# Eight of the 24 modulation slabs move from the first block's attention to the second block's projection

## What is computed

```python
for i in range(DEPTH):                       # DEPTH = 2, dm = 1024
    mod = jax.nn.silu(c) @ mod_w[i] + mod_b[i]          # 1024 x 6144 weights
    modc = jax.nn.silu(c_ctx) @ mod_w[i] + mod_b[i]
    sh1, sc1, g1, sh2, sc2, g2 = jnp.split(mod[:, None, :], 6, axis=-1)
...
    hx = _modulate(_rmsnorm(x, ln1_g[i]), sh1, sc1)
    hc = _modulate(_rmsnorm(ctx, ln1_g[i]), sh1c, sc1c)
    yx, yc = _mixer_ab(...) if i % 2 == 0 else _mixer_cd(...)
    x = x + g1 * yx
    hx = _modulate(_rmsnorm(x, ln2_g[i]), sh2, sc2)
    x = x + g2 * _moe(hx, ...)
```

## Time and profile before

| | |
|---|---|
| median of three runs | 2252.05 us (2248.34 to 2257.75) |
| profiled execution, its own time | 2249.79 us |
| its span | 2248.1 us |
| PE busy | 2137.4 us, 95% |
| DVE busy | 1087.9 us, 48% |
| ACT busy | 613.4 us, 27% |
| DMA | 629.97 MB, mean 280 GB/s |
| first block's attention | about 124 to 223 us |
| second block's projection | about 851 to 905 us |
| second block's attention | about 908 to 946 us |

### The profile page before, as it was taken

How to read it: one execution, slowest core, us unless ns; L and a number is a source line. 1 busy time by engine, 2 the same in 40 slices (tenths; PEclk the granted TensorE clock), 3 DMA queues, 4 the chain that set the end, 5 groups by cost and what they waited for, 6 DMA issues and landing times.

```text
span 2248.1 us, 32119 instructions
## 1 busy us (share of the span) xinstructions
PE 2137.4 (95%) x12440; PEld 1388.0 (62%) x12440; DVE 1087.9 (48%) x1969; ACT 613.4 (27%) x1214; POOL 12.7 (1%) x20
## 2 busy tenths in 40 slices
PE   7999999999999889889999999999999999999998
PEld 4744644444343347564444444478989989898997
DVE  5677541111111136642222222167888777787876
ACT  4446532112121114431111111133451012434001
POOL 0000000000000010000000000000000000000000
PEclk9999999999999999999999999999999999999999
DMA  8189169998999994229999999952345546235452
GB/s 349 76 360 427 75 253 378 386 383 352 429 392 429 428 386 184 113 91 384 427 429 429 428 429 428 427 243 104 140 170 187 187 153 255 110 114 206 181 190 98
DMA packets 50146, 629.97 MB, mean 280 GB/s; under 512 B 5888, under 2 KB 6912, under 8 KB 11904
## 3 DMA queue, kind: packets, MB, share of 16 engines
q1 hardware_dynamic: 45008, 611.30, 66.7%
q10 hardware_dynamic: 2880, 9.44, 1.0%
q0 software_dynamic: 2160, 7.87, 0.9%
HBM read 614.42 MB, written 14.16 MB: 280 GB/s over the span
## 4 chain that ended last, share of the span: by engine, by line
PE 71%; DMA 15%; DVE 10%; ACT 2%; issue 2%; SPq 1%; DVEq 0%; ACTq 0%
PE ps L1908 10%; DMA ring<-in_ex_gate 7%; PE ps L1847 7%; DMA ring<-in_ex_up 6%; PE ps L1376 6%; PE ps L1378 6%; PE ps L1377 6%; PE ps L1987 4%; PE ps L1989 4%; PE ps L1988 4%; PE ps L1924 3%; PE ps L1803 3%; PE ps L1881 2%; PE ps L1723 1%; PE ps L1399 1%
## 5 line engine op out<-in xcount | busy, mean ns | idle before, releaser
L1908 PE MATMUL ps<-ring,E 128*64 128x512 f32 x1152 | 260.1, 609 | 16.7 <-DMA ring<-in_ex_up 14.4
L1378 PE MATMUL ps<-hn_hi,w_lo 128*128 128x256 f32 x928 | 262.4, 283 | 0.0
L1847 PE MATMUL ps<-ring,E 128*64 128x512 f32 x992 | 221.1, 598 | 10.5 <-DMA ring<-in_ex_gate 7.5
L1908 PEld LDWEIGHTS ps<-ring,E 128*64 128x64 f32 x1152 | 87.9, 140 | 185.6 <-issue 185.6
L2736 DVE TENSOR_TENSOR E<-E,ps 128x512 f32<-128x512 f32 x18 | 12.4, 688 | 354.3 <-PE ps L1908 354.3
L1378 PEld LDWEIGHTS ps<-hn_hi,w_lo 128*128 128x128 f32 x928 | 177.8, 192 | 0.0
L1847 PEld LDWEIGHTS ps<-ring,E 128*64 128x64 f32 x992 | 73.8, 138 | 142.3 <-issue 142.1
L1102 ACT ACTIVATE hT<-ps 128x512 f32<-128x512 f32 x70 | 41.9, 599 | 370.1 <-PE ps L1803 370.1
L1376 PE MATMUL ps<-hn_hi,w_lo 128*128 128x256 f32 x480 | 138.3, 288 | 1.7 <-DVE w_lo L2838 1.7
L1377 PE MATMUL ps<-hn_lo,w_lo 128*128 128x256 f32 x480 | 135.7, 283 | 0.0
L2838 DVE TENSOR_TENSOR w_lo<-ring,w_hi 128x4096 fp32r<-128x4096 f32 x30 | 132.8, 4426 | 1.0
(11 more groups left out here) (557 smaller groups left out, 3847.0 us busy)
## 6 DMA issues: line engine op xcount, KB each, us to landing
ring<-in_ex_up SPq DMA_DIRECT2D x64, 2048.0 KB, 16.0
ring<-in_ex_gate SPq DMA_DIRECT2D x62, 2048.0 KB, 16.6
ring<-in_ex_down SPq DMA_DIRECT2D x60, 2048.0 KB, 14.8
ring<-in_w_layer SPq DMA_DIRECT2D x56, 2048.0 KB, 8.2
ring<-in_w_static SPq DMA_DIRECT2D x33, 2048.0 KB, 17.0
y_rows<-E ACTq DMA_DIRECT2D x36, 256.0 KB, 8.4
ring<-in_ex_down SPq DMA_DIRECT2D x8, 1024.0 KB, 16.2
E<-in_w_layer SPq DMA_DIRECT2D x2, 2048.0 KB, 13.0
```

The lines of the kernel that those rows point to most:

```text
L1378: return pe.matmul(out, lo, xhi, start=False, stop=last)
L1847: ins = pe.matmul(ps[half(u), 2 + w, :], xg[:, k, half(u)], weights, start=k == 0, stop=k == KC - 1)
L1908: ins = pe.matmul(ps[half(u), 2 + w, :], xg[:, k, half(u)], slab(2 * w + u, (KC, DE))[:, k, :], start=k == 0, stop=k == KC - 1)
```

## The change

- The table of sets gets a fourth: (0, 4), (4, 12), (12, 16), (16, 24). The first block's attention now sums slabs 5 to 15, one in each of the steps 0 to 10.
- Slabs 16 to 23 are summed in the second block's projection, into PSUM bank 4: after the third and the fourth chunk of queries, after each of the four pooled chunks, after the keys, and between the two halves of the values. The three time-passing matmuls are gone.
- SP loads the second block's six slabs into other slots: four at once with slabs 16 to 18, then 19 to 23 one by one, each when the slab three before it has been summed, then the two out-projection slabs. The guessed expert slabs follow, in another order.
- ACT copies the new row (`late_row`) after the values. PE turns it to columns after the first scores. DVE adds bias and forms scale2 after the first pair's maxima (`modulation_late`). PE waits for that before the first values, which use bank 4.

```diff
-        MOD_SETS = ((0, 4), (4, 12), (12, 24))
-        MOD_PLACE = ((5, 0, 8), (6, 0, 16), (6, 64, 24))
-        MOD_AT = {s: 5 + n for n, s in enumerate(s for s in range(1, 25) if s % 5 != 3)}
+        MOD_SETS = ((0, 4), (4, 12), (12, 16), (16, 24))
+        MOD_PLACE = ((5, 0, 8), (6, 0, 16), (6, 64, 8), (4, 0, 16))
+        MOD_BANK = (6, 7, 7, 4)
+        MOD_AT = {s: 5 + n for n, s in enumerate(range(1, 23, 2))}
...
+        CD_SLOT, CD_COUNT = (0, 1, 2, 2, 5, 3), (1, 1, 2, 2, 3, 4)
+        LATE_MODS = range(16, 24)
+        LATE_SLOT = {j: 3 + (j - 16) % 3 for j in LATE_MODS}
...
+            def second_loads():
...
+                for n in range(4):
+                    cd_load(n)
+                for j in LATE_MODS[0:3]:
+                    late_mod(j)
                 sp.wait_ge(h_ready, 3 * KC)
                 sp.dma_start(invcnt, invcnt_in).then_inc(invcnt_ready, 16)
+                for j in LATE_MODS[3:8]:
+                    sp.wait_ge(mod_mm, j - 2)
+                    late_mod(j)
+                for n, j in ((4, 21), (5, 22)):
+                    sp.wait_ge(mod_mm, j + 1)
+                    cd_load(n)
...
+                    act.wait_ge(mod_mm, 24)
+                    act.activation(late_row, ps[:, 4, :], ACT.Copy).then_inc(mod_ev, 1)
...
+                        if c == 2:
+                            pe.wait_ge(xu_ready, NTM)
+                        if c >= 2:
+                            mod_sum(3, 14 + c)
...
                     pooled(0)
+                    mod_sum(3, 18)
...
                     ins.then_inc(proj_mm, 1)
+                    mod_sum(3, 19)
                     pooled(1, ((0, qss, 3), (5, turn, 2)))
+                    mod_sum(3, 20)
                     pooled(2, ((1, qss, QC), (7, turn, 3)))
+                    mod_sum(3, 21)
                     pooled(3)
+                    mod_sum(3, 22)
                     bank_free(9)
                     values(w1, (0, 1))
                     qrot(g0 + QC, QC)
+                    mod_sum(3, 23)
                     values(w1, (2, 3)).then_inc(proj_mm, 1)
                 if full:
                     mod_sum(1, 4)
-                else:
-                    spin(3, 4)
...
                 if not full:
                     scores(units[0])
+                    mod_columns(3)
                 for s in range(len(units) + 2):
+                    if s == 2 and not full:
+                        pe.wait_ge(mod_ready, 3)
...
+            def modulation_late():
+                dve.wait_ge(mod_fold, 4)
+                link(mod_bias(3))
                 mod_scale(scale2, 1, 32, "ln2_g").then_inc(mod_ready, 1)
```

More of the change, by code:

```diff
@@ L457, in hybrid_program @@
         ab_used.update({HO[0]: (out_mm, 4), HO[1]: (out_mm, 8)})
-        AB_LOADS = [0, 1, 2, 3, IN, HI[0], HI[1], IN + 1, IN + 2, IN + 3] + list(range(4, 24)) + [OUT, OUT + 1, HO[0], HO[1]]
-        AB_FREED = [0, 1, 2, 3, IN, IN + 1, IN + 2, IN + 3, HI[0], HI[1]] + list(range(4, 24)) + [OUT, OUT + 1, HO[0], HO[1]]
+        AB_LOADS = [0, 1, 2, 3, IN, HI[0], HI[1], IN + 1, IN + 2, IN + 3] + list(range(4, 16)) + [OUT, OUT + 1, HO[0], HO[1]]
+        AB_FREED = [0, 1, 2, 3, IN, IN + 1, IN + 2, IN + 3, HI[0], HI[1]] + list(range(4, 16)) + [OUT, OUT + 1, HO[0], HO[1]]
         AB_SLOT, AB_COUNT, ring_loads, ring_user = {}, {}, [0] * RING, [None] * RING
@@ L481, in hybrid_program, with cd_slab @@
         AB_HIGH, AB_SPLIT = (0, 8, 12, 16, 18), (0, 12, 16, 20, 22)
-        cd_slabs = [piece(30 + j) + (used,) for j, used in enumerate(
-            ((proj_mm, 18), (proj_mm, 24), (proj_mm, 23), (pool_mm, 1), (out_mm, 12), (out_mm, 16)))]
-        stream_b = cd_slabs
-        NB_ = len(stream_b)
-        assert NB_ == RING
+        cd_pieces = [piece(30 + j) for j in range(6)]
+        CD_SLOT, CD_COUNT = (0, 1, 2, 2, 5, 3), (1, 1, 2, 2, 3, 4)
+        CD_LOADS = (1, 1, 2, 4, 3, 3)
+        LATE_MODS = range(16, 24)
+        LATE_SLOT = {j: 3 + (j - 16) % 3 for j in LATE_MODS}
+        LATE_COUNT = {j: (j - 16) // 3 + 1 for j in LATE_MODS}
+        cd_freed = [(0, (proj_mm, 18)), (1, (proj_mm, 24)), (4, (mod_mm, 24)), (2, (pool_mm, 1)), (5, (out_mm, 12)), (3, (out_mm, 16))]
+        def cd_slab(n):
+            _, (kk, w) = cd_pieces[n]
+            at = 2048 if n == 3 else 0
+            return ring[:, CD_SLOT[n], at:at + kk * w].rearrange("p (k w) -> p k w", k=kk)
         def slab(n, shape):
@@ L759, in _ @@
             sp.wait_ge(yg_in[NTM - 1], 32)
-            static_loads(stream_b)
-            expert_stream(1, [(r, stream_b[r][2]) for r in range(RING)])
+            second_loads()
+            expert_stream(1, cd_freed)
             for i in range(2):
@@ L1038, in block1 @@
                     for at in (2 * s, 2 * s + 1) if full else ():
-                        if MOD_AT.get(at) in (11, 23):
+                        if MOD_AT.get(at) in (11, 15):
                             act.wait_ge(mod_mm, MOD_AT[at] + 1)
@@ L1363, in take_ab, with take_cd, take_late @@
                 return slab(AB_SLOT[x], STATIC[x])
-            def take_cd(r):
-                pe.wait_ge(slab_in[r], 16 * (ring_loads[r] + 1))
-                return slab(r, stream_b[r][1])
+            def take_cd(n):
+                r = CD_SLOT[n]
+                pe.wait_ge(slab_in[r], 16 * (ring_loads[r] + CD_COUNT[n]))
+                return cd_slab(n)
+            def take_late(j):
+                r = LATE_SLOT[j]
+                pe.wait_ge(slab_in[r], 16 * (ring_loads[r] + LATE_COUNT[j]))
+                return slab(r, STATIC[j])
             def spin(count, bank):
@@ L1390, in mod_sum @@
             def mod_sum(q, j):
-                w = take_ab(j)
+                w = take_ab(j) if q < 3 else take_late(j)
                 j0, j1 = MOD_SETS[q]
@@ L1398, in mod_sum @@
                     u = k % 4
-                    ins = pe.matmul(ps[32 * u:32 * u + 32, 6 if q == 0 else 7, :], condv[:, k, at:at + 32], w[:, k, :], start=j == j0 and k < 4, stop=j == j1 - 1 and k >= 4)
+                    ins = pe.matmul(ps[32 * u:32 * u + 32, MOD_BANK[q], :], condv[:, k, at:at + 32], w[:, k, :], start=j == j0 and k < 4, stop=j == j1 - 1 and k >= 4)
                 ins.then_inc(mod_mm, 1)
@@ L1405, in mod_columns @@
                 for m in range(4):
-                    ins = pe.matmul(ps[:, bank, at + n * m:at + n * m + n], mrow[:, m * P:m * P + P], cc("fold")[:, 0:n], start=True, stop=True)
+                    row = mrow if q < 3 else late_row
+                    ins = pe.matmul(ps[:, bank, at + n * m:at + n * m + n], row[:, m * P:m * P + P], cc("fold")[:, 0:n], start=True, stop=True)
                 ins.then_inc(mod_fold, 1)
@@ L2520, in block1 @@
                         dve.reciprocal(sm[:, u, 0:k], sm[:, u, 0:k]).then_inc(sums_ready, 1)
+                    if s == 0 and not full:
+                        modulation_late()
                     if full:
```

21 lines of the change are left out of this document (12 added, 9 removed).

## The result

| | before | after |
|---|---|---|
| median | 2252.05 us, five runs (2248.34 to 2257.75) | 2273.41 us, five runs (2269.09 to 2275.75) |
| ratio after to before, 95% | | 1.0086 (1.0071 to 1.0100) |
| profiled execution | 2249.79 us, span 2248.1 | 2273.86 us, span 2272.1 |

A forecast was written before the change was run, and what follows sets the result against it. DVE was taken to set the first attention's pace, PE only its crowded steps, and PE the second projection. 13.6 us added less 5.7 gained made 7.9 us slower, 2260.0 us from the median; range 2254 to 2267 us.

The forecast's parts named there:

- The first attention, 5.7 us gained: First block's attention: removing eight slabs gains 4.1 us of DVE's waits plus 1.6 us at step 12.
- the 4.1 of DVE's waits: First attention: DVE's 4.8 us of waits for scores, less 0.67 us in step 0, would go.
- a bound of 6.8: First attention: the 5.7 us gain would be wrong if crowded PE steps stayed above 6.8 us; 6.6 us was expected.
- rival 1: First attention's end: longer PE pause keeps the clock low, costing 4.4 us; net 12.3 us slower, 2264.4 us; chance 0.14.
- A slab in the second projection, 1.77 us: Second block's projection: PE pays each of eight added slabs in full, 1.77 us each, 14.2 us in all.
- The end of that stage, -1.1 us: Second projection's end: without the three time-passing matmuls, the turned keys are copied 1.1 us sooner; bounds 0 and 1.3.
- Bias and scale on DVE, 0.5 us: Second attention's start: one bias and one scale on DVE between the first two pairs add 0.5 us; bounds 0 and 0.7.
- The turn to columns and the new wait, nothing: Second attention: PE's 0.96 us turn of the late row is covered, and its wait before the first values costs nothing.
- The loads, nothing: Second projection: slab loads land in 8.2 us with over 10 us available, so PE waits for none.
- Rival 2: Second projection: slabs fill hidden gaps in PE, so only gains remain, -6.3 us, 2245.8 us; chance 0.09.
- Rival 3: Second projection: loads take 17.0 us, so slabs 19 to 23 each hold PE about 1 us, +5, 2265 us; chance 0.05.
- Rival 4: First attention: step 11's slab counts too and steps get shorter; net +5.5 us, 2257.5 us; chance 0.09.

The follow-up runs named there:

- before12: The kernel before with 5 time-passing matmuls in step 12 of the first attention; 2254.17 us, ratio 0.9994.
- fill12b: The changed kernel with 8 time-passing matmuls in step 12 of the first attention only; 2265.33 us, ratio 1.0038 to the kernel before.
- after2: The changed kernel run once more, unaltered; 2272.55 us, ratio 1.0074 to the kernel before.
- grouped: The changed kernel with the second projection's eight slabs in four places instead of eight; 2269.47 us, ratio 1.0076 to the kernel before.
- fill2: The changed kernel with time-passing matmuls in steps 6 to 12 of the first attention and 4, 6, 7 of the second; 2263.78 us, ratio 1.0052.
- dummy: The changed kernel with the removed slabs' PE work put back in the first attention, without their loads; 2269.88 us, ratio 1.0066 to the kernel before.
- order1: The kernel before with only its step table changed: second slabs of steps 2 and 3 go to steps 0 and 1; 2248.95 us, ratio 0.9979.
- best: order1 with time-passing matmuls in steps 7, 10, 12 of the first attention and 4, 6, 7 of the second; 2247.12 us, ratio 0.9973.

## Why the prediction was wrong, step by step

**The first attention, 5.7 us gained: wrong by its last step.** The 5.7 us themselves were right in sum. before12 and fill12b compare like with like, since both have the fall behind step 2 and the full clock from then on: 100.54 and 95.16 us, 5.4 gained. The split is a little other than said. The last scores stand 6.0 us earlier after the turn of the keys (83.85 and 77.82 us), but the values of step 12 wait for ACT and come 1.6 us later after them (7.33 and 8.97): 4.4 us for the 4.1 of DVE's waits. From there to the last values it is 1.0 us less (3.90 and 2.92), where 1.6 had been read off rows at a fallen clock. One sign of being wrong was met as well, the crowded step of 6.98 us for a bound of 6.8, but in fill12b the same step takes 6.68.

The step that failed is the one that left the clock of the last steps as it was: the longer pause before the values of step 12 stood in the sum with nothing, and rival 1 got 0.14. I had its mechanism, its place and its price: 1.8 us more pause, the channel sums at the lower clock. It gives back 4.4 us by my sum. Measured against the 95.2 us of fill12b it is 5.0 us in after2 and 6.6 in the first profile, where the falls at 192 and 206 us came on top; the values and turns of two steps before the sums ran at half clock too. The evidence against it was one pause without a fall, from 144 to 147 us. The later profiles show what that was worth: at just that place the clock fell in eight of ten. One pause that did no harm in one execution is no proof that it can't. The Trainium skill, TensorE: Matmul & The Clock Gate, section "HAM oscillation", says that pauses past some length leave the next piece cold; the pauses of 3.86 and of 4.14 us at step 12 in the two profiles of the changed kernel agree, and so does the one of 4.14 us in grouped, where only about one row and a half was cold; equal pauses of 2.29 us went both ways.

**A slab in the second projection, 1.77 us: the term was mis-sized.** Measured, 15.2 us in the stage and 1.1 us saved at its end make 16.3 us for eight slabs, 2.04 each. The 1.77 was the share in a pair of slabs, whose price at the joins fell on two. The earlier trace rows shows only a pair; the same trace has isolated slabs too, and there the higher price could have been read:

```profile
198.78 1.92 PE L1399 MATMUL ps<-ring,condv 128*32 128x512 f32 x16
```

The next row starts at 200.63 us, so this one takes 1.85. The shortfall is 2.1 us.

**The end of that stage, -1.1 us: right.** From the last values, which start at 901.37 us before, to the copy of the turned keys it took 907.30 - 901.37 = 5.93 us, and it takes 925.67 - 920.83 = 4.84: 1.1 us less.

**Bias and scale on DVE, 0.5 us: right** (0.42 in the row, 0.46 in the stage of fill2). **The turn to columns and the new wait, nothing: right.** The second attention's own fall of the clock, 1.8 us between the two profiles, stood in no term and in no rival: I asked for the clock only where the pause grew.

**The loads, nothing: right.** They land in 7.9 us for the 8.2 taken, no slab row waits, and in dummy their absence in the first block brings nothing that shows. **Rival 2** (hidden room) is refuted: the pitch was the better evidence, PE had none. **Rival 3** (late slab) didn't occur. **Rival 4** (more is gained) was true only up to the last scores, 5.2 to 6.0 us for the 4.1 counted; the wait for ACT behind them takes the excess back.

**The range.** Rival 1 alone with 12.3 us gave 2264.4. With the joins (+2.1) and the second attention's clock (+1.8) it would have been 16.2 us, 2268.3, against 19.4 us by the ratio and 21.4 by the medians. Of the 18.6 us in the rows of the table the account is: 7.9 said, 6.9 in the first attention, 2.1 for the slabs, 1.8 in the second attention. The rest isn't assigned: it lies in the stages that no edit touches, which differ by 5.4 us between the two profiles. The upper end, 2267, was built from 15.9 us for the second block and 2.3 us gained in the first. Both failed. The 15.9 us left out my own upper bound of a slab, 2.39 us, so the joins had no room in it, and the two stages cost 17.5. The 2.3 us took 3.4 us off for "the half" of rival 1, whose half is 2.2 and whose whole is 4.4; measured, 1.2 us was lost there.

**What becomes of a gain later.** A gain ahead of the first experts reaches them whole: from the out-projection to the first expert matmul it is 82.8 us in every kernel. Behind 550 us PE waits for expert weights while the DMA engines are full, in the kernel before as in order1; a window of the kernel before:

```profile
550.00:600.00 50.00, 46.36 (x210) 20.50 (x208) 7.18 (x22) 7.94 (x10) 0.00 (x0) 0.93 1.01 429
```

The waits of PE from 305 to 860 us (total, times, longest), of before:

```profile
PE ps L1908 <- DMA ring<-in_ex_up: 14.4, 6, 4.1
```

And of order1:

```profile
PE ps L1908 <- DMA ring<-in_ex_up: 17.9, 6, 3.6
```

The first query chunk of the second block started 0.6 us sooner in order1's profile and 3.7 us sooner in best's, where the first expert matmul had been 3.5 and 4.9 us sooner. That stage took 541.2 to 544.9 us over all profiles, so how much of a gain it keeps can't be read from one of them; the medians of order1 and best (-0.21% and -0.27%, 4.7 and 6.1 us) speak for most of it.

## What to carry to other kernels

Taking work from an engine that waits for others makes its pauses longer, and on PE the clock may take back more than the work cost: price the stretch behind each pause also at half clock, and fill the pause with matmuls that do nothing before judging the change. A pause that did no harm in one profile says little: look at the same place in several. Price a small piece by how it will stand, alone or joined to its kind, not by its share of a larger group. When a gain comes from lightening a few crowded steps, first try to move the work by a step or two within the stage; here a table of 19 numbers gave most of that gain and the move into a full stage cost 15 us.

## What the runs showed of the hardware

- The granted clock after one and the same pause is not fixed. Behind the 2.29 us of step 2 it fell in eight of ten profiles (0.63 over 4 us in before12, 1.5 us lost) and stayed at 1.00 in two; behind 2.29 us at step 12 it fell in before and in dummy and not in order1. Behind 3.86 and 4.14 us it was 0.50 to 0.52 for 12 us in two profiles, and behind another 4.14 us (grouped) 0.63 in one window of 4 us and then 1.00: against fill12b the stage is 5.0 us longer in after2 and 1.1 in grouped, with the same pause. Where time-passing matmuls left 0.7 to 0.8 us of a pause, it was 1.00 behind it in every profile.
- Going from full-width f32 matmuls to 32-column tiles and back costs 0.33 us a join: about 0.10 us in the row ahead, 0.10 in the row behind, and 1.85 for 1.76 us in the slab. A slab of 1.76 us costs 2.05 us when it stands alone.
